# The second layer's context projection done inside the first latent retrieval, and read back through DRAM

## The reference, cut to what matters

```python
hc = ctx * (1 + mods_c[1]) + mods_c[0]
proj_c = hc @ (w_in[l][:, :SCAN_COLS] if last else w_in[l])
xh_c, b_c, c_c, dtf_c, dtb_c = ssd_prepare(proj_c[..., :SCAN_COLS], conv_w[l], conv_b[l])
y_c, hf_c, hb_c = bidir_ssd(xh_c, b_c, c_c, dtf_c, dtb_c, a_log[l], dt_bias[l], h0, h0, not last)
```

## Time and profile before

| | us |
|---|---|
| median of three runs | 5154.55 |
| lowest and highest | 5147.31, 5160.57 |
| the profiled execution | 5163.03 |
| its span | 5161.2 |
| PE busy, and its share | 3601.9, 70% |
| DVE busy, and its share | 3258.4, 63% |
| POOL busy, and its share | 2269.7, 44% |
| ACT busy, and its share | 1493.0, 29% |

### The profile page before, as it was taken

How to read it: one execution, slowest core, us unless ns; L and a number is a source line. 1 busy time by engine, 2 the same in 40 slices (tenths; PEclk the granted TensorE clock), 3 DMA queues, 4 the chain that set the end, 5 groups by cost and what they waited for, 6 DMA issues and landing times. The chain is left out here.

```text
span 5161.2 us, 49285 instructions
## 1 busy us (share of the span) xinstructions
PE 3601.9 (70%) x16024; PEld 1846.3 (36%) x16024; DVE 3258.4 (63%) x6632; ACT 1493.0 (29%) x3674; POOL 2269.7 (44%) x1699
## 2 busy tenths in 40 slices
PE   7888888886677975555455557978987555555555
PEld 5576424332266421111111126877843111111111
DVE  5254676664465467776767757557356767677675
ACT  2342344343142222222222223243222222222221
POOL 3253444443033245555555543333324555555554
PEclk8888899998688987777777778988998777777777
DMA  5435999998603699999999972102259999999998
GB/s 184 164 119 214 383 372 397 398 426 362 237 1 111 253 393 418 415 424 413 415 421 406 423 288 67 67 17 81 83 199 360 422 411 417 418 411 415 416 409 373
DMA packets 248273, 1574.53 MB, mean 305 GB/s; under 512 B 41920, under 2 KB 45504, under 8 KB 61760
## 3 DMA queue, kind: packets, MB, share of 16 engines
q0 software_dynamic: 184320, 1342.26, 63.0%
q1 hardware_dynamic: 63696, 229.12, 12.2%
HBM read 1555.38 MB, written 15.89 MB: 304 GB/s over the span
## 5 line engine op out<-in xcount | busy, mean ns | idle before, releaser
L2224 PE MATMUL banks<-arena 128*64 128x512 f32 x5120 | 1639.8, 780 | 1196.8 <-ACT arena L2077 1196.2
L1875 POOL DMA_INDIRECT arena<-in_experts,arena x1280 | 1513.1, 1182 | 1622.9 <-PE banks L2224 1358.3
L1963 DVE CUSTOM_DVE_ANT_0 arena<-arena,token_copies 128x1024 f32<-128x1024 f32 x1280 | 1622.0, 1284 | 719.0 <-DMA arena<-in_experts,arena 645.9
L2224 PEld LDWEIGHTS banks<-arena 128*64 128x64 f32 x5120 | 395.3, 171 | 2298.3 <-ACT arena L2077 1654.4
L2070 ACT ACTIVATE arena<-arena 128x2 f32<-128x2 f32 x640 | 131.2, 205 | 1840.2 <-DVE arena L1963 1832.3
L281 POOL TENSOR_TENSOR wide_low<-wide_blocks,wide_high 128x1024 fp32r<-128x1024 f32 x152 | 381.5, 2532 | 597.4 <-ACT wide_high L271 597.4
L2077 ACT ACTIVATE arena<-arena 128x64 f32<-128x64 f32 x1280 | 376.2, 340 | 292.1 <-POOL arena L1762 251.7
L319 PE MATMUL banks<-activation_a,wide_high 128*128 128x256 f32 (+1 forms) x896 | 317.8, 355 | 8.5 <-ACT arena L343 2.7
L321 PE MATMUL banks<-activation_a,wide_low 128*128 128x256 f32 (+1 forms) x896 | 307.6, 343 | 0.0
L2125 PE MATMUL banks<-arena,wide_blocks 128*128 128x512 f32 (+1 forms) x768 | 296.8, 532 | 2.6 <-ACT arena L1994 2.6
L2178 PE MATMUL banks<-arena,wide_blocks 128*128 128x512 f32 x576 | 275.6, 616 | 0.0
(11 more groups left out here) (240 smaller groups left out, 4953.3 us busy)
## 6 DMA issues: line engine op xcount, KB each, us to landing
wide_blocks<-in_wide SPq DMA_DIRECT2D x170, 1024.0 KB
arena<-in_experts,arena POOLq DMA_INDIRECT x1280
pre_scan<-arena SPq DMA_DIRECT2D x16, 256.0 KB
arena<-pre_scan SPq DMA_DIRECT2D x16, 256.0 KB, 5.3
residual<-in_tokens SPq DMA_DIRECT2D x6, 512.0 KB
arena<-mod_rows SPq DMA_DIRECT2D x6, 512.0 KB
norm_rows<-in_keys SPq DMA_DIRECT2D x3, 1024.0 KB
pre_z<-arena SPq DMA_DIRECT2D x8, 256.0 KB, 7.8
```

Of the source, the lines that this page charges most:

```text
L1875: pool.indirect_dma_start(out=v.ring[:, g % RING], out_offset=None, in_=io["experts"], in_offset=bass.IndirectOffsetOnAxis(ap=c.idx[:, u % ...
L1963: last = nc.vector.tensor_tensor_reduce(out=u_row, in0=u_row, in1=k.copies[:, n % NJ], scale=1.0, scalar=0.0, op0=ALU.mult, op1=ALU.add, a ...
L2224: mm = nc.tensor.matmul(k.ps[j * QUAD:(j + 1) * QUAD, a + half], v.lhs[:, g % 4, j], v.ring[:, (g * NJ + j) % RING, D + half * BANK:D + (h ...
```

## The change

The latent retrieval of the first layer gets the `project` thread too. There it projects the context tokens of the second layer: only x, B and dt (twelve tiles and one dt item, 13 items), from six wide blocks instead of the eight that the projection stage read, with plain float32 matmuls. Their results go to `pre_scan` and `pre_dt` in DRAM. `stage_project(k, 1, CONTEXT, ...)` is gone, and a new stage `stage_return` reads the twelve tiles and dt back, turns them on PE and copies them on ScalarE. The following stages are the same.

```diff
-PRE_WORDS = 7200 + 96
-PRE_BLOCKS = 22
+PRE_WORDS = {2: 7200 + 96, 4: 512 + 64 + 16 + 96 + 256}
+PRE_BLOCKS = {2: 22, 4: 6}
...
+def stage_return(k, layer):
...
+            for m in range(X_TILES):
+                sp.dma_start(tiles[:, m], io["pre_scan"][m, :, 0:T]).then_inc(k.reloaded[0].sem, 16)
+            for m in range(B_TILES):
+                sp.dma_start(v.BT[:, m, 0:T], io["pre_scan"][X_TILES + m, :, 0:T]).then_inc(k.reloaded[1].sem, 16)
+            sp.dma_start(v.hrow, io["hrows"][layer:layer + 1].to_broadcast([P, HR_N])).then_inc(k.loaded.sem, 16)
+            sp.dma_start(v.dt[:, 0:NT], io["pre_dt"][:, 0:NT * 32].rearrange("p (t c) -> p t c", c=32)) \
+                .then_inc(k.loaded.sem, 16)
...
+            for m in range(M):
+                if m == 0:
+                    pe.wait_ge(k.reloaded[0].sem, X + 16 * X_TILES)
+                if m == X_TILES:
+                    pe.wait_ge(k.reloaded[1].sem, B + 16 * B_TILES)
...
+                    last = nc.tensor.transpose(k.ps[:, m % 4, t * P:(t + 1) * P], src[:, t * P:(t + 1) * P], k.ident[:])
...
+                nc.scalar.copy(dst, k.ps[:, m % 4, 0:T].rearrange("p (t c) -> p t c", c=P)).then_inc(k.turn_copied.sem, 1)
...
+    else:
+        v.hT = k.rows[:].rearrange("p a (b c) -> p (a b) c", c=CTX_LEN)
+        v.upad = spare[:, 0:2 * (CTX_LEN + 4)].rearrange("p (a c) -> p a c", a=2)
...
-    PRE, ITEM = proj_at(M) + 8.0, 13.0
+    PRE, ITEM = proj_at(M) + 8.0, (8.0 if short else 13.0)
...
-    Z_ITEMS, FIRST_Z = 8, 1 + SCAN_TILES
-    ITEMS = FIRST_Z + Z_ITEMS + 20
+    PRE_SCAN = X_TILES + B_TILES if short else SCAN_TILES
+    Z_ITEMS, FIRST_Z = 8, 1 + PRE_SCAN
+    ITEMS = FIRST_Z if short else FIRST_Z + Z_ITEMS + 20
...
+            if not (ahead and short):
+                sp.wait_ge(k.s_proj.sem, nth(k.s_proj, M))
+                rows_in()
...
+                if short:
+                    rows_in()
...
-                for m in range(SCAN_TILES):
+                for m in range(PRE_SCAN):
...
-                        u = v.upad[:, m % 2, j:j + SEQ]
+                        u = v.upad[:, m % 2, j:j + AT]
...
-                                       k.ps[:, 4 + (n % 2 if t and not ahead else 0)]).then_inc(k.copy_ready.sem, 1)
+                                       k.ps[:, 4 + (n % 2 if t and two_banks else 0)]).then_inc(k.copy_ready.sem, 1)
...
+                if t == 1 and ahead and short:
+                    pe.wait_ge(k.pre["evac"].sem, pre0["evac"] + ITEMS)
...
-        plan += blocks(1, (W_SCAN, W_Z), *mixer, queries)
+        plan += blocks(1, (W_SCAN, W_SCAN + PRE_BLOCKS[4]), *mixer, queries)
...
-        w = stage_peer(k, 0, LATENT, w, False)
-        w = stage_project(k, 1, CONTEXT, w, False)
+        w = stage_peer(k, 0, LATENT, w, False, ahead=True)
+        stage_return(k, 1)
```

More of the change, by code:

```diff
@@ L1430, in stage_reload, with _ @@
     return w0 + mods.count
+def stage_return(k, layer):
+    nc, io = k.nc, k.io
+    T, NT = CTX_LEN, CTX_LEN // P
+    v = mixer_views(k)
+    tiles = k.arena[:, A_HT:A_HT + X_TILES * T].rearrange("p (m c) -> p m c", m=X_TILES)
+    X, B = k.reloaded[0].base, k.reloaded[1].base
+    ld = k.loaded.base
+    M = X_TILES + B_TILES
+    with nc.Block() as block:
+        @block.sync
+        def _(sp):
+            for m in range(X_TILES):
[5 more added lines that the diff above has]
+                .then_inc(k.loaded.sem, 16)
+            sp.wait_ge(k.loaded.sem, ld + 32)
+        @block.tensor
+        def _(pe):
+            for m in range(M):
[3 more added lines that the diff above has]
+                    pe.wait_ge(k.reloaded[1].sem, B + 16 * B_TILES)
+                src = tiles[:, m] if m < X_TILES else v.BT[:, m - X_TILES]
+                if m >= 4:
+                    pe.wait_ge(k.turn_copied.sem, k.turn_copied.at(m - 3))
+                for t in range(NT):
+                    last = nc.tensor.transpose(k.ps[:, m % 4, t * P:(t + 1) * P], src[:, t * P:(t + 1) * P], k.ident[:])
+                last.then_inc(k.turned.sem, 1)
+        @block.scalar
+        def _(act):
+            for m in range(M):
+                act.wait_ge(k.turned.sem, k.turned.at(m + 1))
+                dst = (v.xtok[:, 0:NT, m * P:(m + 1) * P] if m < X_TILES
+                       else v.Btok[:, 0:NT, (m - X_TILES) * P:(m - X_TILES + 1) * P])
+                nc.scalar.copy(dst, k.ps[:, m % 4, 0:T].rearrange("p (t c) -> p t c", c=P)).then_inc(k.turn_copied.sem, 1)
+    k.loaded.advance(32)
+    for x, n in zip(k.reloaded, (X_TILES, B_TILES)):
+        x.advance(16 * n)
+    for x in (k.turned, k.turn_copied):
+        x.advance(M)
 def box_means(k, dve, plane, win, ROWS, COLS, pa, pb, ra, rb, icnt, tmp, more):
@@ L1797, in stage_peer @@
     M = 2 * PEER_HEADS
-    N_BLOCKS = PEER_HEADS + (PRE_BLOCKS if ahead else 0)
+    N_BLOCKS = PEER_HEADS + (PRE_BLOCKS[NT] if ahead else 0)
+    short = NT == 4
+    ahead_layer, ahead_stream = (1, CONTEXT) if short else (0, LATENT)
+    AT, ab = (CTX_LEN, 0) if short else (SEQ, 2)
+    AN = AT // P
     ld, r0 = k.loaded.base, k.landed[0].base
@@ L1817, in stage_peer @@
     copy_at = lambda n: FIRST + 13.0 + 3.0 * n if n < 2 * NJ else dot_at(n // (2 * NJ) * PEER_HEADS * TOPK - 1) + 5.0
+    two_banks = short or not ahead
     freed_at = lambda q: dot_at(2 * q + 1) + 4.0
@@ L2026, in project @@
                     if e == 0:
-                        nc.scalar.copy(v.stage[:, 0, 0:P], bank[:, 0:P]).then_inc(k.pre["out"].sem, 1)
+                        nc.scalar.copy(v.stage[:, 0, 0:AN * 32], bank[:, 0:AN * 32]).then_inc(k.pre["out"].sem, 1)
                         act.drain().then_inc(k.pre["evac"].sem, 1)
@@ L2153, in project @@
                 pe.wait_ge(k.cols_loaded.sem, k.cols_loaded.at(64))
-                for t in range(4):
+                for t in range(AN):
                     for kt in range(KT):
@@ L2193, in copies @@
                         yield copy_at(n)
-                        if t and not ahead and n >= NJ * 2 + 2:
+                        if t and two_banks and n >= NJ * 2 + 2:
                             pe.wait_ge(k.copy_ready.sem, k.copy_ready.at(n - 1))
@@ L2201, in copies @@
                                 last = nc.tensor.matmul(
-                                    k.ps[q * QUAD:(q + 1) * QUAD, 4 + (n % 2 if t and not ahead else 0), quarter * P:(quarter + 1) * P],
+                                    k.ps[q * QUAD:(q + 1) * QUAD, 4 + (n % 2 if t and two_banks else 0), quarter * P:(quarter + 1) * P],
                                     v.h2T[:, half * 4 + quarter, tokens], k.ident[:], start=True, stop=True)
```

37 lines of the change are left out of this document (21 added, 16 removed).

## The result

The changed kernel takes 5096.09 us (median of 4 runs, 5081.53 to 5106.41) against 5152.22 of the kernel before: ratio 0.9887, 95% interval 0.9858 to 0.9917. Forecast were 5108 and a gain of 46 us; the gain is 56 us in this comparison, and 53 and 43 us in two later ones. The profiled execution has a span of 5104.6 us.

A forecast was written before the change was run, and what follows sets the result against it. DMA was taken to bound the gather plateaus, with the projection between them alone on the path. -79.4 + 28 + 5.1 = -46.3 from 5163.0 gives 5116.7 profiled, 5108 median; range 5094 to 5124, 8 in 10 5088 to 5136.

The forecast's parts named there:

- The place of the gain: Second layer's context projection, ahead of the states stage: nothing runs beside it, so all 94.4 us are on the path.
- The return stage: New stage between the gather's end and the states: 12 to 18 us, 15 taken; net of the removed projection -79.4 us.
- The bytes: Latent retrieval's gather: 7.9 MB more of weight blocks and stores cost 18.8 us at 421 GB/s, the floor.
- VectorE's chain: Latent retrieval's gather: 10.9 us per item against 7.8, 37 us over twelve items; with the floor 18.8, middle 28 taken.
- the precedent: First layer's context retrieval, where the same code already runs 16 such items beside 86 gathers; sum 15.9 against real 15.7.
- The start: Latent retrieval's start: VectorE's first instruction waits for four loads instead of one, +5.1 us (3 to 6).
- The cheap edits: Later row loads, PE's evacuation wait, first weight block's rounding, next stage's modulation: 0, with 3 us as the modulation's end.
- The signs: V-sum pairs 18 to 40 take 130 to 148 us instead of 111, DVE over 0.75 busy, granted clock 0.85 or more.
- B: Latent retrieval's gather: the 7.9 MB fit in for some 5 us, total 5085; chance 0.10.
- C: Latent retrieval's gather: ScalarE's convolution waits delay gelus and V sums, 12.8 us per item, +60, total 5140; chance 0.14.
- E: Latent retrieval's gather: TensorE becomes the bound at the low clock, 16.4 us per item, +103, total 5183; chance 0.07.
- D: Latent retrieval's gather: convolutions hold up GpSimd's gather starts, +30 us, total 5138; sign: indirect DMAs over 1.25 us; chance 0.04.

## Why the prediction was right, step by step

*The place of the gain* was right: the removed stage was all on the path, and its 94.4 us are gone.

*The return stage* was mis-sized: 15 us forecast with 12 as its lower end, 11.4, 12.2 and 11.9 measured. The first transpose came at 6.1 us, near the lower end of 6.0 (the last of the eight loads had landed by then, 2.9 us after its issue), and the tiles took 4.4 to 5.3 us where I had taken 6. The last landing, which I had put at 11 to 12, set no end: VectorE started with the next stage, 0.3 us after ScalarE's last copy. Net -81.3 in the means instead of -79.4.

*The bytes* were right: 18.8 us forecast as the floor, 18.1 left where VectorE was relieved by leaving convolutions out (19.8 up to gelu 80), and 21.8 up to gelu 80 where they were spread.

*VectorE's chain* was the right mechanism, sized too large: 10.9 us per item forecast, while the pairs of stores in the changed kernel follow each other 19.3 us apart (1894.9 to 1991.5 for five; 19.8 in the two later traces), 9.7 to 9.9 us per item, against 7.8 us for as many gathers before. It waited less for ScalarE than in the precedent: 8.5 us over 11 items, 0.8 each (10.8 and 8.8 us in the later traces), not 2.2. The check of this sum against the precedent (15.9 against 15.7) could hardly fail, since the busy time and the waits of one engine add up to the stretch by themselves; whether the waits carry over to items of half the width was the open question, and they didn't. The cost from gelu 18 to 64 is 24.9 us against the 28 taken. The middle between two ends was not argued well, and that it came near is partly luck: the two costs aren't averaged, the longer one shows, and it was VectorE's. This is shown from both sides: taking its work away gives 7 us, and taking bytes away gives 1. It is not the whole of it, since with both reduced some 5 us stand above the bytes.

*The start* was right: 5.1 us forecast, 5.8 in the table, and removing the wait gives back 5.9.

*The cheap edits* stayed within 2 us each where a row could show them: states to the last retrieval +1.9 in the means. What they don't cover are the 7.2 us behind the last item, forecast as 0.

So a forecast of -46.3 stands against -40 by stages, -37.8 between the traced executions, and -43 to -56 between medians. That the forecast lies within the last is in part luck: the unforeseen 7.2 us behind the last item and the 3 us too many for the gather's cost pull in opposite directions, and the medians themselves scatter by 13 us.

*The signs.* The stretch from pair 18 to 40 takes 129.3, 130.9 and 131.5 us in the three traces (130 to 148 named), VectorE is 0.83 busy in the first, and the granted clock is 0.90 to 0.92.

*The rivals.* B (bytes hidden, 5085) is out: with VectorE relieved, DMA goes at 424 GB/s and 18 us remain. C (ScalarE's waits add up, 12.8 us per item) is out: 9.7 to 9.9, and ScalarE waited 3.2 us in all for convolutions. E (TensorE at the low clock) is out: the clock rose to 0.92, PE was busy 102 of 130 us.

D, the port rule, doesn't show. The mean of GpSimd's indirect DMAs was 1258 ns in the first trace of the changed kernel, over the 1.25 us that I had named as the sign of D. The second trace of the same kernel has, in the same stretch:

```profile
L1946 POOL DMA_INDIRECT arena<-in_experts,arena x46 | 52.7, 1146 | 72.1 <-PE banks L2297 64.6 <-issue 7.5
```

The third has 1153 ns, and the three traces of before have 1194, 1233 and 1228: the mean scatters by more than 100 ns between executions of one kernel, and by these three and three it is, if anything, shorter with the convolutions. So the sign was a poor one, and the 1096 ns with most convolutions left out prove nothing either. GpSimd stood 58 to 65 us waiting for PE in that stretch. The rule of the Trainium skill (SBUF — State Buffer, "Who interferes with whom") is neither borne out nor refuted by this; a price of 30 us on the path is ruled out, since the cost up to gelu 80 is 26.2 us in all and 19.8 of them stay with four of five convolution instructions left out.

## What to carry to other kernels

When work moves under a stage that is full of transfers, write down for each engine and for the DMA what an item of it and what the work beside it take; here the longest of these was the cost, within 5 us, and not their sum or a mean. Spreading the same items over more of the stage costs one number in the planner and took away 4 of the 7 us that exceeded the bytes. When such a change is judged by a stretch of the trace, the stretch must end behind the last of its bytes, or what has only moved looks like a gain. A sign that is to tell a rival must be larger than its scatter in the unchanged kernel, which one trace doesn't give. And look at which waits the first instruction of the enlarged stage has inherited: here loads that were needed 190 us later held it up by 5 us.

## What the runs showed of the hardware that I had not expected

- A busy share of DMA near 1 doesn't tell the rate: at 1.01 it moved 412 GB/s with VectorE late and 421 to 422 with VectorE in time, and at 0.97, with fewer bytes to move, 380. The GB/s tell what moved.
- The issue of a small load (48 KB, `pcols`) behind the keys' 1 MB and a scattered column load takes SyncE 3.8 to 4.4 us, where its neighbours take 0.43. It happens in each retrieval with the third thread, in all the traces.
- Eight loads of 128 KB were landed and seen by PE 6.1 us after the first issue, eight of 256 KB 8.5 us after.
